# A two-block transformer kernel: the expert stage's token rows leave DRAM, and 0/1 matrices on TensorE sort and mix them

## What is computed

```python
xb = xt[tok]
hmid = jax.nn.silu(xb @ w_gate[e]) * (xb @ w_up[e])
return (hmid @ w_down[e]) * wt[:, None].astype(xb.dtype)
...
out = jnp.zeros((t, d), xn.dtype).at[slot_token].add(ys.reshape(-1, d))
```

## Time and profile before

| what | value |
|---|---|
| median of 3 runs | 1899.09 us (1896.09 to 1899.28) |
| profiled execution, its own time | 1900.7 us |
| its span | 1899.0 us |
| TensorE busy | 77% of the span |
| DVE, ACT, POOL busy | 40%, 16%, 28% |
| DMA | 599.92 MB, mean 316 GB/s |
| mean granted TensorE clock | 0.887 of full speed |

### The profile page before, as it was taken

One profiled execution on the slowest core, in us unless ns is written; L12 is line 12 of the kernel. 1 busy time (PEld: TensorE's weight loads), 2 busy tenths in 40 slices (PEclk: granted clock), 3 DMA queues, 4 the chain that ended last, 5 costly groups with the idle time before them and its releaser, 6 DMA issues.

```text
span 1899.0 us, 16137 instructions
## 1 busy us (share of the span) xinstructions
PE 1456.3 (77%) x5617; PEld 789.0 (42%) x5617; DVE 768.0 (40%) x1714; ACT 310.8 (16%) x609; POOL 525.8 (28%) x576
## 2 busy tenths in 40 slices
PE   6999995787767777874989999925674949577497
PEld 5626864232222322321665786922232424233243
DVE  2697015000010000002355212987658494855804
ACT  3013113001010010001124102131111203112110
POOL 1003000000000000000000000467777777767773
PEclk9999997888998888887989999967887979798799
DMA  9579743799999999998430135589999999999995
GB/s 309 204 262 406 276 167 143 267 396 396 399 395 396 398 396 398 396 395 297 175 115 1 56 111 199 215 324 409 409 409 409 409 409 409 409 408 409 409 410 235
DMA packets 214020, 599.92 MB, mean 316 GB/s; under 512 B 12386, under 2 KB 18371, under 8 KB 213765
## 3 DMA queue, kind: packets, MB, share of 16 engines
q1 hardware_dynamic: 130484, 295.83, 41.8%
q0 software_dynamic: 81168, 294.92, 39.4%
q10 hardware_dynamic: 2306, 8.40, 1.1%
HBM read 574.45 MB, written 24.65 MB: 315 GB/s over the span
## 4 chain that ended last, share of the span: by engine, by line
PE 54%; DMA 25%; DVE 8%; issue 4%; POOL 4%; SPq 3%; ACT 2%; ACTq 0%; DVEq 0%; POOLq 0%
PE psum L370 35%; PE psum L901 17%; DMA ring<-in_w_up_dram 17%; DVE scratch L1947 5%; DMA ring<-in_peer_v_dram,attnT 5%; SPq L976 3%; POOL ring L1103 3%; DMA ring<-in_peer_u_dram,attnT 2%; ACT actT L1140 1%; PE psum L379 0%; DMA arena<-moe_rows_out,sloti 0%; PE psum L754 0%; DVE ring L1806 0%; DVE ring L1808 0%; DVE scratch L1807 0%
## 5 line engine op out<-in xcount | busy, mean ns | idle before, releaser
L901 PE MATMUL psum<-ring,arena 128*128 128x512 f32 x960 | 428.9, 610 | 213.1 <-DMA ring<-in_peer_v_dram,attnT 213.1
L370 PE MATMUL psum<-ring,arena 128*64 128x512 f32 (+1 forms) x1552 | 395.9, 664 | 126.0 <-DMA ring<-in_w_gate_dram 63.6
L1947 DVE CUSTOM_DVE_ANT_0 scratch<-ring,psum 128x1024 f32<-128x1024 f32 x256 | 309.6, 1220 | 174.0 <-DMA ring<-in_peer_u_dram,attnT 163.8
L901 PEld LDWEIGHTS psum<-ring,arena 128*128 128x128 f32 x960 | 187.7, 196 | 453.6 <-issue 322.2
L1103 POOL DMA_INDIRECT ring<-in_peer_u_dram,attnT x256 | 240.3, 939 | 420.7 <-DVE attnT L1921 315.5
L370 PEld LDWEIGHTS psum<-ring,arena 128*64 128x64 f32 (+1 forms) x1552 | 134.2, 153 | 376.4 <-issue 374.7
L370 PE MATMUL psum<-actT,ring 128*128 128x256 f32 (+1 forms) x1424 | 263.1, 346 | 5.9 <-ACT actT L1140 4.3
L1103 POOL DMA_INDIRECT ring<-in_peer_v_dram,attnT x256 | 244.7, 956 | 79.6 <-issue 61.6
L370 PEld LDWEIGHTS psum<-actT,ring 128*128 128x128 f32 x1424 | 233.4, 193 | 33.2 <-issue 6.9
L1730 DVE TENSOR_TENSOR arena<-arena,psum 128x512 f32<-128x512 f32 x16 | 11.0, 687 | 372.0 <-PE psum L370 372.0
L1080 POOL DMA_DIRECT2D scratch<-moe_rows_in x16 | 8.5, 530 | 493.3 <-PE psum L664 493.3
(11 more groups left out here) (328 smaller groups left out, 1141.9 us busy)
## 6 DMA issues: line engine op xcount, KB each, us to landing
ring<-in_w_up_dram SPq DMA_DIRECT2D x32, 2048.0 KB, 21.0
ring<-in_w_down_dram SPq DMA_DIRECT2D x32, 2048.0 KB, 19.4
ring<-in_w_gate_dram SPq DMA_DIRECT2D x32, 2048.0 KB, 20.0
ring<-in_w_in_dram SPq DMA_DIRECT2D x15, 2048.0 KB, 13.3
ring<-in_ada_w_dram SPq DMA_DIRECT2D x12, 2048.0 KB, 12.9
moe_rows_in<-kdup POOLq DMA_DIRECT2D x21, 512.0 KB, 23.9
scratch<-moe_rows_in POOLq DMA_DIRECT2D x17, 512.0 KB, 6.6
ring<-in_w_out_dram SPq DMA_DIRECT2D x4, 2048.0 KB, 9.3
```

What stands on the lines that cost most here:

```text
L370: return nc.tensor.matmul(o, lhsT, rhs, start=(k == 0), stop=(k == n - 1))
L901: last = nc.tensor.matmul(psum[:, 4 + 2 * t + n, :], diag[:, i, :], row_buf(b)[:, n * 512:(n + 1) * 512], start=first, stop=final)
L1947: V.tensor_tensor_reduce(dotjunk[:, i % 2, :], row_buf(b), x, 1.0, 0.0, ALU.mult, ALU.add, dots[:, t, k:k + 1]).then_inc(ev("dotted"), 1)
```

## The change

`xs` and `ys` are gone, with all their DMAs: the zeros, the four indirect stores, a load and a store of 512 KB in each step, and the four gathers. In their place:

- **Sorting**: for each step DVE writes `pairx`, for each of the two token tiles a 128x128 matrix of 0 and 1 that says which token goes to which of the step's 128 slots (compare a row of 0..127, `iota`, with the token's slot less 128 per step, `slotrel`). `rows_T` is now 16 matmuls (8 column blocks times 2 token tiles) instead of 8 transposes.
- **Mixing back**: DVE writes `pairw`, the same with the weights `picks` in place of the ones; TensorE transposes it (2), ACT copies it out (`pairT`), and after the down matmuls 4 matmuls of 128x512 spread `yrow` over the 256 tokens into banks 3, 4, 7 and 2. DVE adds the four banks to `resid` in every step.
- **Moved**: the two copies of each `ckv` bank go from DVE to ACT; the 5 small operations that make `picks` go behind the slots; the `ckT` transposes and the copies `keys_dup` that read them go behind the expert stage. ACT's queue and POOL have no DMA in the stage any more.

The weights, their ring and SP's waits are as they were, but for one wait on the gathers that is gone.

```diff
@@ tensor @@
-            def rows_T():
-
-                for c in range(KD):
-                    last = nc.tensor.transpose(psum[:, c // 4, (c % 4) * BOTH:(c % 4 + 1) * BOTH], xrow[:, c * P:(c + 1) * P], ident[0:BOTH, 0:BOTH])
-                last.then_inc(ev("rowsT_full"), 1)
+            def rows_T(c0, c1):
+
+                for c in range(c0, c1):
+                    for t in range(NT):
+                        last = mm(psum[:, c // 4, (c % 4) * BOTH:(c % 4 + 1) * BOTH], xcols[:, t, c, :], pairx[:, t, :], t, NT)
+                return last
...
             with pe.Fori(0, n_iter) as i:
 
                 landed_both(0, i)
                 pe.wait_ge(ev("rowsT_ready"), i + 1)
+                pe.wait_ge(ev("mixed"), 4 * i + 1)
                 both(3, xT, 0, slice(0, FF), KD, "gate_full")
                 landed_both(2, i)
+                pe.wait_ge(ev("mixed"), 4 * i + 2)
                 both(4, xT, 2, slice(0, FF), KD, "up_full")
-                pe.wait_ge(ev("rows_in"), 16 * i + 32)
-                pe.sem_inc(pe_step, 1)
-                rows_T()
+                pe.wait_ge(ev("pairx_ready"), 2 * i + 4)
+                rows_T(0, 5)
                 pe.wait_ge(ev("hid_ready"), i + 1)
+                pe.wait_ge(ev("mixed"), 4 * i + 4)
                 pe.sem_inc(pe_step, 1)
...
                 last.then_inc(ev("hidT_full"), 1)
+                pe.wait_ge(ev("pairw_ready"), 2 * i + 2)
+                pe.wait_ge(ev("mixed"), 4 * i + 3)
+                pe.sem_inc(pe_step, 1)
+                for t in range(NT):
+                    last = nc.tensor.transpose(psum[:, 7, t * P:(t + 1) * P], pairw[:, t, :], ident[:, :])
+                last.then_inc(ev("pairT_full"), 1)
+                rows_T(5, KD).then_inc(ev("rowsT_full"), 1)
                 landed_both(4, i)
                 pe.wait_ge(ev("hidT_ready"), i + 1)
                 for n in range(2):
-                    pe.wait_ge(ev(f"down_read{n}"), i + 1)
                     both(5 + n, hidT, 4, slice(n * 512, (n + 1) * 512), 4, f"down_full{n}")
...
+                pe.wait_ge(ev("pairT_ready"), i + 1)
+                for n in range(2):
+                    pe.wait_ge(ev(f"y_ready{n}"), i + 1)
+                    for t in range(NT):
+                        mm(psum[:, MIX_BANK[n, t], :], pairT[:, t * P:(t + 1) * P], yrow[:, n * 512:(n + 1) * 512], 0, 1) \
+                            .then_inc(ev("mix_full"), 1)
@@ scalar @@
+                act.wait_ge(ev("pairT_full"), i + 1)
+                nc.scalar.activation(pairT, psum[:, 7, 0:T], ACT.Copy).then_inc(ev("pairT_ready"), 1)
                 act.wait_ge(ev("down_full0"), i + 1)
-                act.wait_ge(ev("stored"), 16 * i + 1)
-                nc.scalar.activation(yrow[:, 0:512], psum[0:BOTH, 5, :], ACT.Copy).then_inc(ev("down_read0"), 1)
-                act.wait_ge(ev("down_read0"), i + 2)
-                act.wait_ge(ev("down_read1"), i + 2)
-                act.dma_start(ys[bass.ds(i * BOTH, BOTH), :], yrow).then_inc(ev("stored"), 16)
+                nc.scalar.activation(yrow[:, 0:512], psum[0:BOTH, 5, :], ACT.Copy).then_inc(ev("y_ready0"), 1)
@@ vector @@
+            def pair_rows(slots, built):
+
+                for t in range(NT):
+                    V.tensor_scalar(pairx[:, t, :], iota[:, :], slots[:, 2 * t:2 * t + 1], None, ALU.is_equal).then_inc(ev("pair_step"), 1)
+                dve.wait_ge(ev("pair_step"), built + 2)
+                for t in range(NT):
+                    V.scalar_tensor_tensor(pairx[:, t, :], iota[:, :], slots[:, 2 * t + 1:2 * t + 2], pairx[:, t, :],
+                                           ALU.is_equal, ALU.add).then_inc(ev("pairx_ready"), 1)
...
                 V.tensor_tensor(hrow, silu, psum[0:BOTH, 4, :], ALU.mult).then_inc(ev("hid_ready"), 1)
+
+                dve.wait_ge(ev("slots_moved"), i + 1)
+                for t in range(NT):
+                    V.tensor_scalar(pairw[:, t, :], iota[:, :], slotrel[:, 4 + 2 * t:5 + 2 * t], picks[:, 2 * t:2 * t + 1],
+                                    ALU.is_equal, ALU.mult).then_inc(ev("pair_step"), 1)
+                    V.tensor_scalar(wtmp[:, t, :], iota[:, :], slotrel[:, 5 + 2 * t:6 + 2 * t], picks[:, 2 * t + 1:2 * t + 2],
+                                    ALU.is_equal, ALU.mult).then_inc(ev("pair_step"), 1)
+                dve.wait_ge(ev("pair_step"), 6 * i + 8)
+                for t in range(NT):
+                    V.tensor_tensor(pairw[:, t, :], pairw[:, t, :], wtmp[:, t, :], ALU.add).then_inc(ev("pairw_ready"), 1)
+
                 rows_out(i + 2)
+                pair_rows(slotrel, 6 * i + 8)
+                dve.wait_ge(ev("pairx_ready"), 2 * i + 6)
+                V.tensor_scalar(slotrel[:, :], slotrel[:, :], float(BOTH), None, ALU.subtract).then_inc(ev("slots_moved"), 1)
+
                 dve.wait_ge(ev("down_full1"), i + 1)
-                dve.wait_ge(ev("stored"), 16 * i + 1)
-                V.tensor_copy(yrow[:, 512:1024], psum[0:BOTH, 6, :]).then_inc(ev("down_read1"), 1)
-
-
-            for j in range(4):
-                dve.wait_ge(ev("fetched"), 16 * 4)
-                r = resid[:, j // 2, :]
-                v(V.scalar_tensor_tensor(r, back[:, j, :], picks[:, j:j + 1], r, ALU.mult, ALU.add), "moe_added" if j % 2 else None)
+                V.tensor_copy(yrow[:, 512:1024], psum[0:BOTH, 6, :]).then_inc(ev("y_ready1"), 1)
+                for n in range(2):
+                    for t in range(NT):
+                        r = resid[:, t, n * 512:(n + 1) * 512]
+                        dve.wait_ge(ev("mix_full"), 4 * i + (2 * n + t + 1))
+                        dve.wait_ge(ev("mixed"), 4 * i + (2 * n + t + 1))
+                        V.tensor_tensor(r, r, psum[:, MIX_BANK[n, t], :], ALU.add).then_inc(ev("mixed"), 1)
```

More of the change, by code:

```diff
@@ L32 @@
 MAXSTEPS = (EXPERTS + EXTRA) // 2
-ROWS = (EXPERTS + EXTRA) * CAP
 PH, PKEYS, PTOP = 8, 128, 16
@@ L177, in build @@
         hrow = arena1[0:BOTH, 2048:2560]
-        back = arena2[:, :].rearrange("p (a d) -> p a d", d=D)
+        pairx = arena2[:, 1280:1536].rearrange("p (t c) -> p t c", t=NT)
+        pairw = arena2[:, 1536:1792].rearrange("p (t c) -> p t c", t=NT)
+        wtmp = arena2[:, 1024:1280].rearrange("p (t c) -> p t c", t=NT)
+        pairT = arena2[:, 1792:2048]
+        xcols = scratch[:, :, :].rearrange("p t (k q) -> p t k q", k=KD)
+        hcols = hrow.rearrange("p (k q) -> p k q", k=4)
+        xgain = colsA[:, 36:44]
+        MIX_BANK = {(0, 0): 3, (0, 1): 4, (1, 0): 7, (1, 1): 2}
         zs = arena1[:, 0:3072].rearrange("p (c t) -> p c t", t=T)
@@ L1053, in _ @@
             pool.dma_start(wroute[:, :, GROUPS:], A["w_expert"][0].rearrange("(k p) n -> p k n", p=P)).then_inc(ev("bcast_in"), 16)
[L1055 to L1071, removed]
-            pool.wait_ge(ev("sent"), 16 * 2 * NT)
-            pool.dma_start(xrow, xs[0:BOTH, :]).then_inc(ev("rows_in"), 16)
-            pool.wait_ge(ev("trips_ready"), 1)
-            n_iter = pool.value_load(trips[0:1, 0:1], min_val=STEPS, max_val=MAXSTEPS)
-            with pool.Fori(0, n_iter) as i:
-                pool.wait_ge(ev("rowsT_full"), i + 1)
-                pool.sem_inc(pool_step, 1)
-                pool.dma_start(xrow, xs[bass.ds((i + 1) * BOTH, BOTH), :]).then_inc(ev("rows_in"), 16)
-            pool.wait_ge(ev("stored"), n_iter * 16 + 1)
-            pool.sem_inc(pool_step, 1)
-            for j in range(4):
-                pool.indirect_dma_start(out=back[:, j, :], out_offset=None, in_=ys[:, :],
-                                        in_offset=bass.IndirectOffsetOnAxis(ap=sloti[:, j:j + 1], axis=0)).then_inc(ev("fetched"), 16)
             slot_reader = {1: "bx11", 2: "keyT3", 3: "pq01", 4: "pq11", 5: "pq21", 0: "pq31"}
@@ L1245, in _ @@
                 a(nc.scalar.activation(stat("rt_e1")[:, t:t + 1], rt[:, 144 + 8 * t + 1:144 + 8 * t + 2], ACT.Exp, bias=stat("rt_nv")[:, t:t + 1]), "rt_e1")
+            for t in range(NT):
+                ps = full(act, f"ckv{t}")
+                nc.scalar.activation(kvt[:, t * T:t * T + P], ps[:, 0:P], ACT.Copy)
+                last(nc.scalar.activation(vtok[:, 2 + t, :], ps[:, P:2 * P], ACT.Copy), f"ckv{t}")
             act.wait_ge(ev("ck_ss"), 1)
@@ L1252, in _ @@
             n_iter = act.value_load(trips[0:1, 0:1], min_val=STEPS, max_val=MAXSTEPS)
-            act.sem_inc(ev("down_read0"), 1)
-            act.sem_inc(ev("stored"), 1)
             with act.Fori(0, n_iter) as i:
@@ L1700, in _ @@
             for t in range(NT):
-                ps = full(dve, f"ckv{t}")
-                v(V.tensor_copy(kvt[:, t * T:t * T + P], ps[:, 0:P]))
-                last(V.tensor_copy(vtok[:, 2 + t, :], ps[:, P:2 * P]), f"ckv{t}")
+                emptied(dve, f"ckv{t}")
             v(V.tensor_tensor(sqc, kk, kk, ALU.mult))
@@ L1745, in _ @@
             norm_rows("zn", resid, "zn_ready")
+            keys_dup("ckT", T)
             v(V.memset(hpad[:, :, :, 0:1], 0.0))
```

98 lines of the change are left out of this document (46 added, 52 removed).

## The result

| | before | after |
|---|---|---|
| median | 1899.18 us (4 runs, 1896.09 to 1900.18) | 1844.51 us (4 runs, 1841.13 to 1846.57) |
| profiled execution, own time / span | 1900.7 / 1899.0 us | 1845.78 / 1844.0 us |
| mean granted TensorE clock | 0.887 | 0.913 |
| DMA | 599.92 MB | 565.36 MB |

What follows compares the result with a forecast made beforehand. The prediction took the expert steps to be bound by DMA bytes. From 1900.7 us it took 11.0 (start), 43.8 (steps) and 12.9 (tail), giving 1833.0, stated as 1831 us against the runs' median; range 1821 to 1856.

Steps and rivals of the forecast that it cites:

- The case's own range: Whole kernel: the main forecast of 1831 us was given 1821 to 1841 us, with chance 0.62.
- the rival in which TensorE becomes the bound: Expert steps: TensorE's work and clock loss make a step 32.4 to 33.1 us; about 1853 us in all, chance 0.25.
- What bounds the steps: Expert steps: bound by bytes, 13.63 MB in 34.38 us at 396.5 GB/s, not by TensorE.
- The rival of steps that don't shrink: Expert steps: a latency loop stays at 34.4 us, only start and tail gain; 1875 us in all, chance 0.06.
- The rate of weights alone: Expert steps: weights without row transfers move at 400 GB/s, 31.46 us a step, 43.8 us less over 15 steps.
- the bound that the range had: Expert steps: lowest rate allowed, the step's own mean of 396.5 GB/s, 31.7 us a step, 39 us less.
- TensorE keeps up: Expert steps: TensorE's work is 29.4 us at full clock, under 31.46 with 2.1 to spare.
- Its fear for the clock: Expert steps: TensorE keeps losing 3.0 us a step to stretches at its lower clock, 1.2 GHz.
- Start: Up to the first gate matmul: it starts at 328.6 instead of 339.64 us, when its weights land; 11.0 us less.
- Tail: Last up matmuls to the norm's first square: 23.5 us instead of 36.4, 12.9 less.
- Priced at nothing: Writes of zeros dropped, `ckT` and `keys_dup` moved, DVE's four copies: no change; 2 us if the copies' cover failed.
- The rule weighed: Expert steps: an HBM limit of about 358 GB/s gives 35.1 us a step and no gain; the prediction rejected it.

Runs made afterwards that it cites:

- traffic: Changed kernel with a 512 KB load and a 512 KB store that nobody uses put back in each step: 1883.62 us.
- down2k: Changed kernel with each down piece loaded as two halves of its columns, so all contiguous runs are 2 KB: 1854.28 us.
- perm_early: Changed kernel with the count in `mixed` moved earlier, gate and up pieces in 16 KB runs, and normed rows written in matching order for contiguous sorting: 1805.25 us.
- mix2: Changed kernel with each of the four mixing matmuls of a step done twice: 1858.27 us.
- perm_all: Kernel of `perm_early` with the down pieces in 16 KB runs too, hidden rows written in matching order: 1801.30 us.
- early: Changed kernel with DVE's starting increment of `mixed` moved directly behind the first scaling of the sorted rows: 1837.68 us.
- runs_x: Changed kernel with gate and up pieces in 16 KB runs and the sorting reading the tokens' columns strided: 1874.48 us.

## Why the prediction was right, and what was off

The direction and the mechanism were right: the steps were bound by bytes, and they shrank. That the time is inside the stated range is in part luck. The case's own range ended at 1841; the range went on to 1856 for the rival in which TensorE becomes the bound, and that is not what happened. Of the prediction's own signs of being right, the step of 31.4 us at 400 GB/s, the first gate by 330 us released by its weights, and the tail of 23 to 24 us did not come; of its signs of being wrong, one did: transfers of weights alone at 396 GB/s or lower.

**What bounds the steps: right.** The step shrank with its bytes from 34.38 to 31.92 us, and with the bytes put back it is 34.40 (`traffic`). The rival of steps that don't shrink fell with it.

**The rate of weights alone: the largest error.** The mis-sized term is that of the steps, 43.8 us forecast and 35.7 measured, and the step of the prediction that failed is: "In the part of a step with no row transfer in flight the engines move 400 GB/s, in the part that has them 393. I take 400". The rate differs by the length of the runs and not by whether rows move. Slices of 2 us in one step of the kernel before show it. In the first only down pieces move (packets of 3.8 KB in the mean), in the second 2 KB runs beside the load of rows, in the third 2 KB runs beside the store of rows, in the last 2 KB runs alone:

```profile
585.00:587.00 2.00, 2.00 (x8) 0.83 (x6) 0.00 (x0) 0.00 (x0) 0.00 (x0) 0.50 1.02 408
...
597.00:599.00 2.00, 2.00 (x12) 0.85 (x10) 0.00 (x0) 0.40 (x1) 0.00 (x0) 1.00 1.06 399
...
607.00:609.00 2.00, 2.00 (x8) 0.66 (x6) 0.00 (x0) 0.00 (x0) 0.00 (x0) 0.50 1.02 409
...
613.00:615.00 2.00, 2.00 (x12) 0.60 (x10) 0.00 (x0) 0.00 (x0) 0.00 (x0) 1.00 1.06 389
```

With no row transfer in flight the rate is 408 in one and 389 in the other. The 18 us of the earlier trace rows at 400 held both sorts of slice. At 387.5 for 8.39 MB in 2 KB runs and 408 for 4.19 MB in 4 KB runs a step is 21.65 + 10.27 = 31.92 us, which is what was measured; with the 1.05 MB of rows (4 KB runs too) it is 34.49, against 34.38. (Both rates are read from the changed kernel, so its own 31.92 is no test of them; the step before, `down2k` and `perm_early` are.) The rows were the cheap bytes, so taking them away lowered the mean rate, from 396.5 to 394, below the bound that the range had. (That bound is worth 40 us over 15 steps, where the prediction has 39.) Over 13 steps the gain was 32.1 us (411.51 to 858.61 before, 401.26 to 816.24 after) where 38.0 was forecast. The other 2.3 us of this term lie in the first two steps: they gave 3.6 us where 5.8 was forecast, because TensorE works there without a gap from its first gate on (332.94 us, to 400.7) and is their bound in the changed kernel.

**TensorE keeps up: right.** The forecast's 29.4 us per step is 28.96 (`mix2`), and no new piece of work is waited for. The rival in which TensorE becomes the bound gave 1842 to 1863, which holds the time measured, but its mechanism was not there: TensorE waited for an up piece in each step from the third on. Its fear for the clock also failed: it is 0.98 over 13 steps. Two of three up matmuls follow a wait of 2.7 us, and one of these two runs partly at the lower level (8.80 against 7.11 us), which the next wait absorbs: it is 1.05 us instead of 2.75; in `perm_all`, where TensorE has no gap, the granted clock is 1.00 for 408 us.

**Start: a wait was missed.** The forecast had the sorting ready at 326.3 (325.9) and the weights at 328.6 (327.74 in `early`). The failed step is that the prediction walked through these two alone. The change had added a wait on `mixed` ahead of the first gate, and DVE makes this count only behind the next `pairx`, `picks` and the context's keys: 16 operations of DVE, a square root with a table load on ACT (1.28 us), and reading `trips`. Moving the count brought the gate forward by 5.2 us, of which the edit can claim 4.6; the term missed its forecast by 4.3.

**Tail: right, with its own condition.** 24.80 against 23.5 forecast. The prediction said that 3 us hang on whether the last up runs at half clock; it did for part of its time (8.78 against 7.09). In `early` it didn't, and the tail was 23.1.

**Priced at nothing: right.** With `ckT` and `keys_dup` moved behind the stage, what follows it is within 1.0 us. The zeros' going is worth 0.3 us at most: the first step's last piece is issued at 319.92 instead of 320.20.

**The rule weighed.** By the limit of about 358 GB/s that the Trainium skill, "DMA: Bandwidth & Descriptors", "Specifications", states, a step would have been 35.1 us, an estimate from that figure. The traces do not agree: weights moved at 394 GB/s here, and at 428 in `perm_all`. What the same page of the Trainium skill says in "Why small descriptors are slow (HBM only)" bears on it better: every packet carries a fixed overhead. The runs here agree in kind, at lengths far above those that it speaks of: 387, 408 and 428 GB/s at 2, 4 and 16 KB.

The errors add up: 8.1 in the steps, 4.3 at the start, 1.3 in the tail, less 1.0 behind it, 12.7 of the 12.8 us by which the profiled execution lies over the sum of 1833.0.

## What to carry to other kernels

A rate that is read from a window belongs to what moved in it. Before bytes are taken from a full queue, list the contiguous run of each kind of transfer, and cut the windows so that each holds one kind; the bytes that go may be the cheap ones. Where a change adds a wait to the first pass of a loop, walk through everything that is queued ahead of the instruction that answers it: here a count that was true 7 us earlier stood behind unrelated work. And once a transfer-bound loop has given back its bytes, the layout of the rest can be worth as much again: with 16 KB runs and the early count the same kernel takes 1801.30 us, 43 us less than the change alone, 36 of them by the layout; TensorE's work in a step and the time of its bytes are then nearly equal.

## What the runs showed of the hardware

The rate of 16 busy DMA engines depends on the run even at some KB: 387 GB/s at 2 KB (`down2k`, 425 us), about 408 at 4 KB (8 us of one step of the changed kernel, and slices), 428 at 16 KB (`perm_all`, 408 us, busy share 1.01). An estimate from the first two: 2 KB takes one engine 85 ns and 4 KB 161 ns, so a run costs some 9 ns beside its bytes; by it 16 KB runs would move about 425, where 428 was measured.

A stationary operand read with a stride of 32 bytes made the fp32 sorting matmuls of 128x128 twice as long (`runs_x`, 5.03 us against 2.50 for ten); the weight loads' busy time in a step went from 12.45 (`perm_all`) to 16.50 us with it. VectorE lost less by writing with a stride (512 bytes between neighbours): 1.06 us against 0.69 for 128x512.
